# The first group of the middle-sized expert visits: from 176 to 152 token columns

## The reference

```python
def moe_swiglu(x, w_router, w1, w3, w2):
    logits = xf @ w_router
    top_vals, top_idx = lax.top_k(logits, TOP_K)          # 2 of 8 experts
    gates = jax.nn.softmax(top_vals, axis=-1)
    ...
    def expert_block(args):
        xblk, e = args
        h = jax.nn.silu(xblk @ w1[e]) * (xblk @ w3[e])    # 1024 -> 3584
        return h @ w2[e]                                  # 3584 -> 1024
```

## Time and profile before

| | us |
|---|---|
| median of 3 runs | 2094.53 |
| lowest and highest run | 2093.53, 2095.32 |
| the profiled execution | 2092.87 |
| its span, first to last instruction | 2091.0 |
| TensorE busy | 2008.7 (96%) |
| DVE busy, ACT busy | 1545.6 (74%), 1219.1 (58%) |
| experts' part of the span, from TensorE's first expert matmul | from 815.25 |

### The profile page before, as it was taken

The page is one execution under the profiler, slowest core; times in us unless marked ns, Lnnn a source line. Parts: engine busy times, 40 slices in busy tenths (PEclk is TensorE's granted clock), DMA queues, the critical chain, the costliest instruction groups (busy, mean ns, idle before and its releaser), DMA issues.

```text
span 2091.0 us, 33626 instructions
## 1 busy us (share of the span) xinstructions
PE 2008.7 (96%) x11083; PEld 1743.8 (83%) x11084; DVE 1545.6 (74%) x1696; ACT 1219.1 (58%) x1554; POOL 91.0 (4%) x132
## 2 busy tenths in 40 slices
PE   8999999999999998999999999999999999999992
PEld 7777888888897778999999888888998888889991
DVE  6896666656678966766766689898676888987765
ACT  4433555555554424555656577787655777866653
POOL 1000000100000003000000000000000000000002
PEclk9999999999999999999999999999999999999996
DMA  7321766665553214776777699999776999997743
GB/s 221 119 71 57 224 212 213 215 193 189 181 157 123 83 61 162 250 239 223 268 242 252 220 370 378 367 386 340 255 242 207 369 369 364 389 354 243 251 144 135
DMA packets 245442, 488.18 MB, mean 233 GB/s; under 512 B 16724, under 2 KB 86468, under 8 KB 245396
## 3 DMA queue, kind: packets, MB, share of 16 engines
q1 hardware_dynamic: 237668, 462.04, 65.0%
q0 software_dynamic: 7728, 25.52, 3.5%
HBM read 473.20 MB, written 14.30 MB: 233 GB/s over the span
## 4 chain that ended last, share of the span: by engine, by line
PE 81%; DVE 10%; issue 4%; ACT 2%; DMA 2%; POOL 0%; DVEq 0%; POOLq 0%; ACTq 0%; SPq 0%
PE PS L1343 80%; DVE wlo L690 2%; DVE PS L792 2%; DVE OV L766 1%; DMA raw<-in_expert_w 1%; ACT whi L354 1%; DVE OV L780 1%; PE PS L1648 1%; PE PS L1366 0%; DVE OV L796 0%; DVE OV L762 0%; DMA OV<-in_norm_mix_g 0%; DVE OV L713 0%; DMA OV<-y_rows,addr 0%; DVE OV L927 0%
## 5 line engine op out<-in xcount | busy, mean ns | idle before, releaser
L690 DVE TENSOR_TENSOR wlo<-raw,whi 128x1024 fp32r<-128x1024 f32 x882 | 1044.2, 1221 | 198.8 <-ACT whi L354 192.8
L354 ACT ACTIVATE whi<-raw 128x1024 fp32r<-128x1024 f32 x882 | 898.4, 1053 | 224.1 <-PE PS L1343 128.6
L1343 PE MATMUL PS<-XN,whi 128*128 128x512 f32 (+3 forms) x3328 | 955.9, 364 | 17.3 <-DVE OV L927 10.1
L1343 PE MATMUL PS<-XN,wlo 128*128 128x152 f32 (+3 forms) x2944 | 775.9, 264 | 0.0
L1343 PEld LDWEIGHTS PS<-XN,whi 128*128 128x128 f32 x3328 | 619.4, 189 | 84.0 <-DVE wlo L690 14.3
L1343 PE MATMUL PS<-whi,XN 128*128 128x512 f32 x2272 | 669.9, 394 | 8.7 <-DVE XN L801 3.5
L1343 PEld LDWEIGHTS PS<-XN,wlo 128*128 128x128 f32 x2944 | 562.4, 191 | 12.9
L1343 PEld LDWEIGHTS PS<-whi,XN 128*128 128x128 f32 x2272 | 423.6, 188 | 103.4 <-issue 6.9
L1343 PE MATMUL PS<-wlo,XN 128*128 128x512 f32 x1248 | 423.2, 391 | 0.0
L1343 PEld LDWEIGHTS PS<-wlo,XN 128*128 128x128 f32 x1248 | 234.4, 188 | 50.6
L1343 PE MATMUL PS<-whi,hid 128*128 128x512 f32 x384 | 111.6, 392 | 0.8 <-DVE hid L886 0.8
(11 more groups left out here) (200 smaller groups left out, 963.6 us busy)
## 6 DMA issues: line engine op xcount, KB each, us to landing
raw<-in_expert_w SPq DMA_DIRECT2D x672, 512.0 KB, 5.1
raw<-in_ffn_w SPq DMA_DIRECT2D x144, 512.0 KB, 3.5
raw<-in_w_in SPq DMA_DIRECT2D x40, 512.0 KB, 4.8
raw<-in_w_out SPq DMA_DIRECT2D x16, 512.0 KB, 4.3
y_rows<-OV POOLq DMA_DIRECT2D x14, 512.0 KB, 5.3
y_rows<-OV POOLq DMA_DIRECT2D x14, 192.0 KB, 6.4
RES<-in_x SPq DMA_DIRECT2D x4, 512.0 KB, 5.8
x_tok<-OV POOLq DMA_DIRECT2D x4, 512.0 KB, 2.9
```

What stands on the lines that cost most here:

```text
L354: act.activation(whi[:, u0 % CONV, half(h)], raw[:, r, half(h)], ACT.Copy).then_inc(s["hi_done"], 1)
L690: dve.tensor_tensor(wlo[:, w, half(h)], raw[:, u0 % RAW, half(h)], whi[:, w, half(h)].bitcast(F32), ALU.subtract).then_inc(s["lo_done"], 1)
L1343: return pe.matmul(out_, lhsT, rhs, start=start, stop=stop, skip_group_check=True)
```

## The change

Group 0 of a heavy visit gets the class `c` in place of `WIDE`, and so the same choice that the other groups have.

```diff
@@ -1688,7 +1688,7 @@
             def heavy(i, c):
 
                 pe.wait_ge(s["glo_done"], i * 3 + 3)
-                heavy_ups(i, 0, 0, False, WIDE)
+                heavy_ups(i, 0, 0, False, c)
                 with pe.Fori(1, GROUPS) as g:
                     heavy_ups(i, g, -2, True, c)
                     pe.wait_ge(s["hid_ok"], i * GROUPS + g + 1)
```

## The result

| | before | after |
|---|---|---|
| median of the runs of this comparison, us | 2094.03 (4 runs) | 2123.68 (4 runs) |
| ratio, 95% interval | | 1.0145, 1.0132 to 1.0158 |
| the profiled execution, us | 2092.87 | 2125.21 |
| its span, us | 2091.0 | 2123.3 |

The kernel is slower by 30 us, over four times the 6.7 us of the forecast and outside its range of 2093 to 2116. The sign was right, the size was not.

What follows compares the result with a forecast made beforehand. TensorE, busy 96% of the span, was taken as the bound. Visit 0's jump 3.5, light visits 4.4, visit 1 0, visits 4 and 7 -1.2 gave +6.7 us: 2099.6 profiled, 2101.2 median; range 2093 to 2116.

Steps and rivals of the forecast that it cites:

- What bounds the kernel, and which visits the change touches: Whole kernel: TensorE bounds it, busy 96% of the span; the change touches group 0 of visits 1, 4 and 7.
- The columns, -0.58 in each of three visits: Group 0, visits 1, 4, 7: part 0 gains nothing, waiting for DVE's sum; part 1 gains 0.58 us each, -1.74 in all.
- the lost clock: Visit 4 falling to half clock behind its wait: 2.7 us on top of a fitting loop, 2099.0 us; chance 0.05.
- the first rival: The loop's code fits, only visit 0's jump counts besides the columns: +1.8 us, 2096.3 us; chance 0.35 including the lost clock.
- Visit 0's jump, +3.5: Start of visit 0: the new branch jumps over the narrow body to code not loaded, delaying the expert part 3.5 us.
- The half clock at the start: Start of visit 0: the half clock moves along with the first matmul and costs what it cost before.
- the refetch: Loop head: a ninth packet pushes out the head's; each return costs 3.25 us more, about 1.1 idle per light visit, +4.4.
- a lead of 2.3: Starts of visits 1 and 3: the sequencer runs 2.3 us ahead of the first matmul, covering that much of a branch.
- the third rival: Every visit turns the code store over, with a second stall of 3.5 us: +18.8 on the forecast, 2120 us; chance 0.12.
- The edge: Loop's size decides the price: up to eight packets a loss of 2 us at most, beyond it 7 or more.

Runs made afterwards that it cites:

- experiment 1: The changed kernel with eight more filler matmuls ahead of the loop over the visits: 2097.27 us, ratio 1.0010 to the kernel before.
- experiment 10: The kernel of experiment 5 with eight filler matmuls between part 0 and part 1 in group 0's narrow body: 2092.28 us, ratio 0.9981 to the kernel before.
- experiment 5: The kernel of experiment 1 with the wide body first, so class 2 runs on and class 1 jumps: 2092.67 us, ratio 0.9989 to the kernel before.
- experiment 4: The changed kernel with thirty more filler matmuls ahead of the loop: 2139.67 us, ratio 1.0208 to the kernel before.
- 6: The kernel of experiment 5 with the heavy branch also ahead of the light one on TensorE: 2092.83 us, ratio 0.9989 to the kernel before.
- experiment 7: The kernel before with only TensorE's heavy branch put ahead of the light one, no narrow body in group 0: 2100.45 us, ratio 1.0027.

## Why the forecast was right in sign and wrong in size

**What bounds the kernel, and which visits the change touches:** right; the counts by shape are the ones foretold.

**The columns, -0.58 in each of three visits.** Nearly right. Measured without the turnover it is -0.4 in visit 1. That part 0 gains nothing because part 1 waits for DVE's sum is shown by the 0.84 us wait of experiment 1, which was forecast as 0.6; the splits ahead of that sum came 0.3 us later in the visit, behind a weight transfer, and part 1 kept only 0.3 of its 0.58. In visit 4 the longer wait (3.86 us, forecast 3.55) was followed by half clock, and part 1 took 10.6 us where it had taken 8.79. That is the lost clock of the first rival, and visit 7 gave about as much back: part 1 took 10.0 us in place of 11.5. The reason given, the length of the wait, did not hold (experiment 10).

**Visit 0's jump, +3.5.** Right. Line 1683 took 3.30 us, and the first matmul came at 819.84, less 1.27 that lie ahead, 818.57; forecast 818.7. The half clock at the start moved along, as forecast: part 0 took 11.78 us (11.74 before), and group 1 starts 4.64 us later, of which 1.27 lie ahead. But the term can't be won back whole. In the kernel before the half clock of part 0 covered the wait for DVE's sum; with the stall gone and part 0 at full clock (experiment 5) part 1 starts at 826.75, hardly sooner than the 826.99 of before, and the half clock falls on it.

**The step that failed is the refetch.** The forecast put it so: the ninth packet pushes out the one with the loop head, and each return costs 3.25 us less a lead of 2.3, about 1.1 in each light visit, +4.4, and nothing more. (By its own numbers 3.25 less 2.3 is 0.95, +3.8; and the three chances that it counts as slower, 0.42, 0.12 and 0.05, make 0.59 and not 0.57. Neither matters here.) Measured, the visits lose 27.7 us. Two things in it were wrong.

The first is what is lost. When the oldest packet goes first, fetching the head again pushes out the packet behind it, which is needed next, and so on round the loop. One packet too many doesn't cost one fetch a round but all of them. Queue 8 from the end of visit 0 to that of visit 1, on to the end of visit 4, and on to that of visit 7 (1007, 1202, 1640 and 2079 us):

```profile
q8 instruction: 9, 0.15, 0.3%
...
q8 instruction: 9, 0.15, 0.1%
...
q8 instruction: 9, 0.15, 0.1%
```

Nine each time, as many as the eight that the loop touches and the one ahead of its end, once for every heavy visit. The light visits had only the head in the forecast; in the trace they fetch 3 after a heavy visit and none after a light one, presumably because a light visit touches so little that all of it stays. So visits 3 and 6 cost nothing (forecast 1.1 each), and the price falls on the return from a heavy visit and the jump or the run into the next packet behind it: 9.4 us of idling at visit 1, 3.1 and 2.2 in visit 2, 2.7 and 3.0 in visit 5. That is the third rival's mechanism, which had 2120 us and a chance of 0.12. That its time came so near is partly luck: it had the loss in every visit, where only three returns pay, and at 3.5 us, where they took 5.3 to 5.9 and a second wait followed. I argued against it that the light branch's packets had survived 370 us unused. They had, in a loop that fits. In one that doesn't, none of the nine stayed from one heavy visit to the next.

The second is the price of a packet. 3.4 us came from two branches, one where the weights' queue was not full and one behind the last visit, where it was empty. In the loop the weights fill the DMA engines, and a fetch took 5.3 to 5.9 us, or 6.8 with a second packet ahead of it. The other kernels repeat it: with a DMA share of up to 0.83 a branch that waited for a packet took 3.1 to 3.9 us, between 0.84 and 0.90 from 2.6 to 5.8, and with 0.95 and more 4.0 to 7.0, but for one of 3.2 in experiment 4. In all of them the packet's own transfer is short (0.9 to 2.1 us) and the branch ends 1.3 to 1.8 us behind it; the rest is the time before the transfer begins. That the weights in the DMA engines are what delays it is read from this agreement; no run changed the traffic alone. The lead of 2.3 then covers less than half. The half clock behind the longer waits came on top: the matmuls of the visits took 7.4 us longer, the columns' gain already taken off.

By the Trainium skill (Runtime: NRT & Kernel Launch, Instruction fetch mechanics) TensorE's store is 2048 instructions, first in, first out, refilled in blocks of 256. The runs agree: 27 packets between 870 and 2040 us, three times nine, with a loop of 6.7 blocks that touches eight, none with the same loop when it touches seven, and the same again 256 instructions later. The remark in the same section of the Trainium skill that the store is only two lines is not borne out, since experiment 1 went through seven visits without a fetch.

**The edge was misjudged too.** I wrote that the price is decided at the loop's size: up to eight packets a loss of 2 us. By my count of the program the loop has 6.7 packets' worth of instructions. It is the start of the loop in its packet, and the one fetched ahead, that make eight or nine of it. The same loop 32 instructions further on is a loss of 1.5 us (first rival: 1.8).

## What to carry to other kernels

A loop with branches on an engine has a footprint in code packets, and a change that adds a body has to be judged by it: count the packets of the code queue inside the loop before and after, since none there means it fits, and any there that weren't before are the first suspect. When a loop is near the limit, where it starts matters as much as how long it is: a few idle instructions ahead of it can be worth more than the whole optimisation. And a stall that is taken away at the start of a stage is only gained if the next wait of that stage, here DVE's sum behind the weights, does not end at a fixed time, and if the clock holds behind it.

The version to keep is that of experiment 5 or 6: the narrow group 0, eight fillers, the wide body first, 0.1% faster than the kernel before (0.9989, with the interval's upper end at 0.9998) and 1.5% faster than the change as it was made (1.0145 / 0.9989).

## What the runs showed of the hardware that was not expected

- A branch to code that is not there took 3.1 to 3.9 us with a DMA share of up to 0.83 and 4.0 to 7.0 with 0.95 and more (one of 3.2). The packet's own transfer takes 0.9 to 2.1 of it; what grows is the time before the transfer begins, from 0.6 to 1.6 us to mostly 1.6 to 4.1.
- A loop of 6.7 packets stays in place or is fetched anew for every heavy visit, nine packets a time, 30 packets in all or 57, by a shift of 20 instructions at most (three fillers, 1.76% slower than the kernel before; eight, 0.1%).
- Whether a first jump waits depends on where it stands in the packets, not on its length alone: turning one branch of the kernel before round (experiment 7) took away one long jump of 3.7 us and brought two of 4.9 and 5.0, one of them a jump that had taken 0.34.
- TensorE's clock stayed at 1.00 behind a wait of 2.97 us in one kernel and was 0.83 behind one of 2.36 us in another, at the same wait for DVE's sum in visit 4 (one execution each).
